# Second token tile handled in two column halves at three points between sub-layers

## The reference, cut to what matters

```
for i in range(DEPTH):
    a = hybrid_mixer(rmsnorm(h, mix_norm_pre[i]), ...)
    h = h + rmsnorm(a, mix_norm_post[i])
    c = memory_cross_attention(rmsnorm(h, xa_norm_pre[i]), rmsnorm(mem, mem_norm[i]), ...)
    h = h + rmsnorm(c, xa_norm_post[i])
    hn = rmsnorm(h, ffn_norm_pre[i])
    f = swiglu(hn, ...) if i % 2 == 0 else moe_swiglu(hn, ...)   # layer 0 dense, layer 1 top-2 of 8
    h = h + rmsnorm(f, ffn_norm_post[i])
```

## Time and profile before

| | |
|---|---|
| median of 3 runs | 1512.36 us |
| the three runs | 1511.96, 1515.37, 1512.36 us |
| the profiled execution, whole | 1515.45 us |
| its span in the profile | 1513.6 us |
| mean granted TensorE clock in the span | 0.992 of full speed |
| TensorE matmul busy | 1451.1 us |
| VectorE busy | 1128.5 us |
| ScalarE busy | 954.8 us |

### The profile page before, as it was taken

How to read it: one execution, slowest core, us unless ns; L and a number is a source line. 1 busy time by engine, 2 the same in 40 slices (tenths; PEclk the granted TensorE clock), 3 DMA queues, 4 the chain that set the end, 5 groups by cost and what they waited for, 6 DMA issues and landing times.

```text
span 1513.6 us, 21967 instructions
## 1 busy us (share of the span) xinstructions
PE 1451.1 (96%) x8888; PEld 1274.0 (84%) x8888; DVE 1128.5 (75%) x1085; ACT 954.8 (63%) x1116; POOL 177.9 (12%) x133
## 2 busy tenths in 40 slices
PE   8999999999999999998999999999999999999995
PEld 7979988888889889998999777777777899977774
DVE  4766546666666656457777799999999876789996
ACT  5467446334454675355545599999999544579894
POOL 6200000000015000002000203123040300020400
PEclk9999999999999999999999999999999999999999
DMA  9217424455534065425656799999999856679993
GB/s 368 95 49 299 181 91 157 176 189 194 201 122 161 4 250 196 142 96 235 238 223 250 273 375 421 421 421 421 421 421 420 348 225 250 240 284 414 420 422 125
DMA packets 55138, 387.38 MB, mean 256 GB/s; under 512 B 6368, under 2 KB 6624, under 8 KB 9216
## 3 DMA queue, kind: packets, MB, share of 16 engines
q1 hardware_dynamic: 54112, 384.20, 64.6%
q10 hardware_dynamic: 432, 1.08, 0.2%
q0 software_dynamic: 496, 0.74, 0.1%
HBM read 383.90 MB, written 2.10 MB: 255 GB/s over the span
## 4 chain that ended last, share of the span: by engine, by line
PE 64%; DVE 25%; ACT 5%; issue 4%; DMA 0%; SPq 0%; ACTq 0%; DVEq 0%
DVE w_low L1292 15%; PE banks L1794 10%; PE banks L1795 10%; PE banks L1796 10%; PE banks L2121 7%; PE banks L1967 5%; PE banks L2123 5%; DVE low_more L1292 5%; PE banks L1792 4%; PE banks L1793 3%; PE banks L1969 3%; ACT w_high L847 2%; PE banks L2016 1%; DVE after_heads L1575 1%; PE banks L2002 1%
## 5 line engine op out<-in xcount | busy, mean ns | idle before, releaser
L1292 DVE TENSOR_TENSOR w_low<-raw,w_high 128x2048 fp32r<-128x2048 f32 x258 | 587.7, 2294 | 161.6 <-ACT w_high L847 161.4
L847 ACT ACTIVATE w_high<-raw 128x2048 fp32r<-128x2048 f32 x258 | 492.2, 1920 | 162.8 <-PE banks L1969 65.8
L1792 PE MATMUL banks<-w_high,rows 128*128 128x512 f32 (+1 forms) x424 | 161.6, 387 | 3.1 <-ACT after_heads L1116 2.5
L1793 PE MATMUL banks<-w_low,rows 128*128 128x512 f32 (+1 forms) x424 | 156.7, 375 | 0.0
L2121 PE MATMUL banks<-rows,w_high 128*128 128x320 f32 x544 | 143.1, 308 | 3.0 <-ACT high_more L847 2.2
L2123 PE MATMUL banks<-rows,w_low 128*128 128x256 f32 x544 | 142.5, 278 | 0.0
L1794 PE MATMUL banks<-rows,w_high 128*128 128x256 f32 x480 | 137.6, 287 | 1.4 <-DVE rows L1293 1.4
L1794 PE MATMUL banks<-w_high,rows 128*128 128x256 f32 x480 | 137.5, 286 | 0.0
L1795 PE MATMUL banks<-rows,w_high 128*128 128x256 f32 x480 | 136.8, 285 | 0.0
L1796 PE MATMUL banks<-rows,w_low 128*128 128x256 f32 x480 | 136.7, 285 | 0.0
L1796 PE MATMUL banks<-w_high,rows 128*128 128x256 f32 x480 | 135.8, 283 | 0.0
(11 more groups left out here) (237 smaller groups left out, 3257.7 us busy)
## 6 DMA issues: line engine op xcount, KB each, us to landing
raw<-in_pieces_dram SPq DMA_DIRECT2D x291, 1024.0 KB, 7.6
raw_more<-in_pieces_dram SPq DMA_DIRECT2D x66, 1024.0 KB, 9.0
phase<-in_mem_dram SPq DMA_DIRECT2D x2, 1024.0 KB, 6.8
early<-in_constants_dram SPq DMA_DIRECT2D x1, 1088.0 KB, 14.2
h_res<-in_x_dram SPq DMA_DIRECT2D x2, 512.0 KB, 4.7
phase<-in_mix_norm_post_dram SPq DMA_DIRECT2D x2, 512.0 KB, 4.6
phase<-in_xa_norm_post_dram SPq DMA_DIRECT2D x2, 512.0 KB, 6.6
kept<-h_res SPq DMA_DIRECT2D x2, 512.0 KB, 3.1
```

What stands on the lines that cost most here:

```text
L847: return act.activation(out_, in_, ACT.Copy, scale=scale)
L1292: return dve.tensor_tensor(out_, in_, plain(high), ALU.subtract)
L1792: pe.matmul(dst, stay[0], move[0], start=start, stop=False, skip_group_check=True)
L1793: return pe.matmul(dst, stay[0], move[1], start=False, stop=stop, skip_group_check=True)
```

## The change

The second token tile (`t` = 1) at A, B and C goes in two halves of 512 columns. The first token tile, the mixer outputs and all other norms stay as they are.

- VectorE adds columns 0 to 511 first and raises a new semaphore `h_half`, then columns 512 to 1023 and raises `h_ready` as before (`add_halves`).
- ScalarE waits for `h_half`, squares the first half into `part_sums`, turns the sum into a bias with an Identity of one column, waits for `h_ready`, squares the second half, and then runs Ln and Exp as before (`rms_halves`).
- VectorE scales the two halves in two instructions, the first raises a new semaphore `xn_half`, the second `xn_ready`.
- TensorE waits for `xn_half` ahead of the first two banks and for `xn_ready` ahead of the other two.

No DMA is added or moved, and the counts of `h_ready` and `xn_ready` stay what they were, so all else that waits on them waits for the second half.

```diff
+HALVED = [(0, 2), (1, 0), (1, 2)]
...
+        h_half, xn_half = sem("h_half"), sem("xn_half")
...
+            def rms_halves(n, t, src, first_added, all_added):
+                first, second = slice(0, HALF), slice(HALF, D)
+                act.wait_ge(h_half, first_added)
+                chain(act.activation(xn[:, t, first], src[:, t, first], ACT.Square, accum_out=part_sums[:, t, 0:1]))
+                chain(act.activation(part_bias[:, t, 0:1], part_sums[:, t, 0:1], ACT.Identity, bias=eps, scale=1.0 / D))
+                act.wait_ge(h_ready, all_added)
+                chain(act.activation(xn[:, t, second], src[:, t, second], ACT.Square, accum_out=part_sums[:, t, 1:2]))
+                inverse_rms(n, t, part_sums[:, t, 1:2], part_bias[:, t, 0:1])
...
             def pre(layer, q):
                 for t in range(TT):
+                    if (layer, q) in HALVED and t == TT - 1:
+                        rms_halves(norm(layer, 2 * q), t, h_res, HALVED.index((layer, q)) + 1, TT * (3 * layer + q - 1) + t + 1)
+                        continue
...
-            def normed(n, t, dst, src):
-                return dve.tensor_scalar(dst[:, t, :], src[:, t, :], inv_rms(n, t), None, ALU.mult)
+            def normed(n, t, dst, src, at=slice(0, D)):
+                return dve.tensor_scalar(dst[:, t, at], src[:, t, at], inv_rms(n, t), None, ALU.mult)
...
             def pre(layer, q):
                 for t in range(TT):
+                    if (layer, q) in HALVED and t == TT - 1:
+                        normed(norm(layer, 2 * q), t, xn, h_res, slice(0, HALF)).then_inc(xn_half, 1)
+                        normed(norm(layer, 2 * q), t, xn, h_res, slice(HALF, D)).then_inc(xn_ready, 1)
+                        continue
...
+            def add_halves(t, rows, inv):
+                for at, done in ((slice(0, HALF), h_half), (slice(HALF, D), h_ready)):
+                    dve.scalar_tensor_tensor(out=h_res[:, t, at], in0=rows[:, at], scalar=inv, in1=h_res[:, t, at],
+                                             op0=ALU.mult, op1=ALU.add).then_inc(done, 1)
...
-                        add_to_rows(t, res[:, t, :], inv_rms(norm(layer, 2 * q + 1), t))
+                        add = add_halves if stage == "xo" and t == TT - 1 else add_to_rows
+                        add(t, res[:, t, :], inv_rms(norm(layer, 2 * q + 1), t))
...
-            def turn_stage(layer, stage, src, ready, count):
+            def turn_stage(layer, stage, src, ready, count, halved=None):
 
                 for t in range(TT):
-                    pe.wait_ge(ready, count - TT + t + 1)
+                    by_half = halved is not None and t == TT - 1
+                    if by_half:
+                        pe.wait_ge(xn_half, HALVED.index(halved) + 1)
+                    else:
+                        pe.wait_ge(ready, count - TT + t + 1)
                     for i in range(COUNT[stage]):
+                        if by_half and i == COUNT[stage] // 2:
+                            pe.wait_ge(ready, count)
...
-                turn_stage(layer, "mixT", xn, xn_ready, TT * (3 * layer + 1))
+                turn_stage(layer, "mixT", xn, xn_ready, TT * (3 * layer + 1), (layer, 0) if layer else None)
...
-                turn_stage(layer, "ffT", xn, xn_ready, TT * (3 * layer + 3))
+                turn_stage(layer, "ffT", xn, xn_ready, TT * (3 * layer + 3), (layer, 2))
```

More of the change, by code:

```diff
@@ L1473, in take_output @@
                     dve.wait_ge(y_taken, 2 * t + 2)
-                    add_to_rows(t, res[:, t, :], inv_rms(norm(layer, 5), t))
+                    add = add_halves if t == TT - 1 else add_to_rows
+                    add(t, res[:, t, :], inv_rms(norm(layer, 5), t))
             def find_places(e):
```

## The result

The changed kernel took 1521.47 us (median of 8 runs, 1512.98 to 1522.94), the kernel before, beside it, 1515.20 (8 runs, 1511.96 to 1516.83). The ratio is 1.0033, 95% interval 1.0021 to 1.0044: slower by 0.33%, where 1513.5 us and no measurable change had been forecast, and 4.5 us above the top of the range. In two later comparisons it was 1519.18 us at 1.0029 (1.0018 to 1.0040) and 1519.32 us at 1.0037 (1.0023 to 1.0051). Three comparisons agree, so the loss is real: some 4 to 6 us.

What follows compares the result with a forecast made beforehand. The prediction took TensorE, busy 96% of the span, to bound the kernel, with ScalarE the bound at A, B and C. Steps of 0.37, 0.40 and 0.37 us, together 1.14, on 1512.36 gave 1513.5 us, range 1511.2 to 1517.0.

Steps and rivals of the forecast that it cites:

- ScalarE is the bound, not the add: At A, B and C the second Square waits for the add by 0.03 us at most, since ScalarE is still busy.
- 0.67 us a point for the Square in halves: On ScalarE at A, B and C, two half Squares and an Identity take 1.86 us for 1.19.
- the second estimate of the forecast: By the Trainium skill's fixed costs for the added Square and Identity, the change would add 0.47 us a point.
- 0.27 back from the scaling in halves: On VectorE at each point, the first scaled half is done 0.27 us sooner than the whole was.
- The second transposes hidden behind the first four: On TensorE, the first four transposes run from 0.52 to 0.99 us, so the second half is at worst 0.03 late.
- The sum of 1.14 us: Slower by 0.37 us at A, 0.40 at B and 0.37 at C, with bounds from 0.24 to 2.55.
- The pass: The delays at A, B and C all reach the end; at B perhaps only 0.20 of 0.40 us.
- The step that failed: the clock: The 1.14 us sum has no term for TensorE's clock, at its lower level behind B and C, 1.00 at A.
- rival 1: TensorE's clock falls at A as well, costing 3.5 us more, 1517.0 us in all; chance 0.20.
- The base: The median of the runs before, 1512.36 us, to which the forecast added 1.14 us.
- Rival 2: First half's work goes under the second half's add, gaining 0.30 us at A and C, 0.27 at B; chance 0.05.
- Rivals 3 and 4: At later stages and C, delay swallowed, 1512.4 us, chance 0.10; at B or C, one clock fall fewer, 1511.0, chance 0.08.

## Why the prediction was wrong

*ScalarE is the bound, not the add.* Right. ScalarE starts the first half's Square 0.10 to 0.12 us after the start of the first tile's Exp at A, B and C, the pace of two instructions that nothing holds up.

*0.67 us a point for the Square in halves.* Measured 0.64 at A (1.83 for 1.19), so the second estimate of the forecast, 0.47 by the pages' figures, does not hold here. *0.27 back from the scaling in halves.* Measured alone, 0.26 and 0.28. *The second transposes hidden behind the first four.* Right, 1.10 us for the eight. *The sum of 1.14 us.* Measured 0.34 at A, 0.39 at B (10.93 for 10.54) and 0.33 at C (24.61 for 24.28, with the clock low equally long in both): 1.06.

*The pass.* All three delays pass on, as forecast: from A to B it is 185.85 us and from B to C 227.97, without a fall, in traces of either kernel. At C more passed on than the delay itself, which is the step below.

*The step that failed: the clock.* The sum has the added cost of the clock at nothing. The forecast took the falls at B and C as paid for already, "about 7 us at half speed", asked whether one would come back sooner or not come, and on the side of the loss only whether A would get one too (rival 1, 0.20). The runs showed 10.2 us more at the lower level a run, an estimated 2.9 us beside the 1.1 of the steps, most of it at C. Two things were wrong in the forecast's view. The fall at C has no fixed length and no fixed start. In the profiled execution of before it begins at 687.4, 2.1 us into the router's matmuls, and lasts 6.8 us; in three of the five traces with the wider gap at C, not filled, it begins 1.7 to 1.9 us ahead of the router (683.4 for 685.1 in the trace shown) and lasts 20.5 us, into the gathering for the first expert, and that is 4.3 us at C alone. In none of the four traces with the gap as before does it come ahead of the router or last longer than 10.3 us. And the place with a fall already in it was the most endangered, not the safe one: three gaps and then 8-column matmuls follow each other there. The 3.4 us spread of the three runs was in view and was read as "the size of one fall"; it also said that the falls differ from run to run, and 0.3 us more idle time moved most runs to the side of the longer ones. Rival 1 named the mechanism, a fall brought by a wider gap, but put it mainly in the wrong place. "TensorE: Matmul & The Clock Gate" of the Trainium skill (Part 1) ties the clock to recent activity; the runs agree in kind: with 7 fillers in the gap at C the clock is low for 26.2 us a run instead of 37.6.

*The base.* The median of three runs was 2.8 us under that of many. That part of the 8.0 us between 1513.5 and 1521.47 is the chance of a small sample and no fault of the mechanism. The ratio is free of it: 1.0008 forecast, 1.0033 measured.

*Rival 2, the gain looked for,* did not occur, since ScalarE never waits for the half add. The kernel with only the scaling halved gains by another way, without touching the Square. *Rivals 3 and 4* did not occur in the mean. The changed kernel's shortest execution has no fall at B, as rival 4 has it, but so has the second trace of the kernel before, so the later start is not shown to be the reason.

## What to carry to other kernels

Before halving a step to overlap it, ask whether the consumer is waiting for it or is busy with something else: ScalarE was busy with the first tile until the whole add ended, so half an add earlier bought nothing and a second fixed cost was paid. Where the trace shows a fall of TensorE's clock behind a gap, price a delay there not by its own length but by the fall that it may bring forward or lengthen, and take the clock of many runs, not one trace. A cheap cure in this kernel was a few filler transposes in the very gap, sized to end just before the awaited data; it paid for the delay, and a gain over the kernel before came only with the Square left whole.

## What the runs showed of the hardware

- A delay of 0.33 us in a chain of small steps at three places changed the median by 3.4 us (1518.45 for 1515.03); the clock was low for 33.9 us a run, for 27.2 in the 31 runs of the kernel before of the same set.
- During matmuls with 8 moving columns, back to back and shown as 100% busy, the clock fell: 2.1 us into them in the trace of before (687.4 for 685.29), 1.9 in its second, and 2.1 and 2.2 in two of the changed kernel. No idle time of TensorE in the 9 us ahead of the fall was longer than 0.82 us in the trace of before. With the gaps filled it still fell (10.3 us low), and in the one trace with a 128-column filler ahead of each as well it stayed at 1.00.
- Splitting a Square of 1024 columns with a sum in two costs 0.64 us: 0.31 for the fixed part and the second accumulator read, and 0.33 for the Identity that joins the sums. Splitting VectorE's scaling costs 0.13 us (0.88 for 0.75), and the next stage starts 0.26 to 0.28 us sooner (7.58 for 7.84 us at A, 10.26 for 10.54 at B).
